# Latent attention over cached pages: score and value products that take four sequences in turn inside each key piece and page

## The reference

```python
def one(args):                                     # one sample
    pt, ql, qp, cn, kn = args
    cp = ckv_pool[pt].reshape(-1, KV_LORA)         # 4096 x 256, also the values
    kp = kpe_pool[pt].reshape(-1, QK_ROPE)         # 4096 x 32
    s_past = (jnp.einsum('qhc,kc->hqk', ql, cp) + jnp.einsum('qhr,kr->hqk', qp, kp)).astype(jnp.float32) * SM_SCALE
...
    p = jax.nn.softmax(jnp.concatenate([s_past, s_new], -1), axis=-1).astype(cp.dtype)
    return (jnp.einsum('hqk,kc->qhc', p[..., :n_past], cp)
            + jnp.einsum('hqk,kc->qhc', p[..., n_past:], cn))
```

## Time and profile before

| | |
|---|---|
| time, median of 3 runs | 4361.26 us (4354.4 to 4364.62) |
| profiled execution: its span | 4359.5 us (1.8 us under the median) |
| mean granted clock of PE in it | 0.927 of full speed |
| PE busy | 88% of the span |
| DVE / POOL / ACT busy | 63% / 35% / 23% |
| latent-attention tiles with page steps | about 660 to 1058 us from the start |

### The profile page before, as it was taken

How to read it: one execution, slowest core, us unless ns; L and a number is a source line. 1 busy time by engine, 2 the same in 40 slices (tenths; PEclk the granted TensorE clock), 3 DMA queues, 4 the chain that set the end, 5 groups by cost and what they waited for, 6 DMA issues and landing times. The chain is left out here.

```text
span 4359.5 us, 50665 instructions
## 1 busy us (share of the span) xinstructions
PE 3848.5 (88%) x17166; PEld 2860.4 (66%) x17166; DVE 2764.4 (63%) x6184; ACT 1006.0 (23%) x2810; POOL 1544.8 (35%) x1332
## 2 busy tenths in 40 slices
PE   9798958888899989989898789977999899898986
PEld 4477844445777767777676545555777777676765
DVE  0255632222599987877776623335999888877777
ACT  0132201121122255431010112211222455310000
POOL 0011213332035365555554200000263655655553
PEclk9888979899999989999999899968999999899998
DMA  3100056775568799999999674404598999999996
GB/s 129 43 15 17 27 161 186 206 205 165 191 247 335 299 400 417 416 410 379 392 395 389 249 255 167 154 19 156 215 343 309 371 416 417 404 387 392 389 398 257
DMA packets 374218, 1168.40 MB, mean 268 GB/s; under 512 B 36914, under 2 KB 163523, under 8 KB 345994
## 3 DMA queue, kind: packets, MB, share of 16 engines
q0 software_dynamic: 159920, 570.80, 34.3%
q1 hardware_dynamic: 187386, 518.08, 32.7%
q10 hardware_dynamic: 26656, 76.29, 4.6%
HBM read 1091.93 MB, written 68.59 MB: 266 GB/s over the span
## 5 line engine op out<-in xcount | busy, mean ns | idle before, releaser
L2046 POOL DMA_INDIRECT peer_ru<-in_u_rows,peer_expert x512 | 797.8, 1558 | 1697.1 <-DVE peer_expert L2426 831.5
L2124 PE MATMUL peer_bank<-peer_xT,peer_u 128*128 128x288 f32 x4096 | 1032.4, 409 | 1.8 <-ACT peer_held L2251 1.8
L2124 PEld LDWEIGHTS peer_bank<-peer_xT,peer_u 128*128 128x128 f32 x4096 | 775.2, 192 | 208.0 <-issue 3.4
L2345 DVE SCALAR_TENSOR_TENSOR y<-peer_rv,peer_weight,y 128x1024 f32<-128x1024 f32 x512 | 656.4, 1282 | 80.2 <-issue 56.5
L2355 DVE CUSTOM_DVE_ANT_0 peer_ru<-peer_ru,x 128x1024 f32<-128x1024 f32 x512 | 623.2, 1217 | 40.7 <-DMA peer_ru<-in_u_rows,peer_expert 40.1
L2054 POOL DMA_INDIRECT peer_rv<-in_v_rows,peer_expert x512 | 536.0, 1047 | 234.2 <-issue 143.6
L2175 PE MATMUL peer_bank<-peer_u,region 128*128 128x288 f32 x1664 | 428.9, 421 | 62.8 <-DMA region<-in_v 62.8
L2175 PEld LDWEIGHTS peer_bank<-peer_u,region 128*128 128x128 f32 x1664 | 328.1, 198 | 161.0 <-DMA region<-in_v 67.4
L2175 PE MATMUL peer_bank<-region,peer_u 128*128 128x288 f32 x1536 | 376.4, 406 | 0.0
L2197 ACT ACTIVATE peer_act_g<-peer_dot 128x1 f32<-128x1 f32 x512 | 103.6, 202 | 1152.9 <-DVE peer_dot L2355 1143.2
L2494 DVE TENSOR_TENSOR peer_hidden<-peer_hidden,peer_bank 128x288 f32<-128x288 f32 x496 | 220.7, 451 | 228.0 <-PE peer_bank L2175 226.5
(11 more groups left out here) (519 smaller groups left out, 4982.2 us busy)
## 6 DMA issues: line engine op xcount, KB each, us to landing
peer_u<-in_uT SPq DMA_DIRECT2D x128, 1024.0 KB, 8.5
peer_u<-in_v SPq DMA_DIRECT2D x32, 2048.0 KB, 12.6
region<-in_v SPq DMA_DIRECT2D x32, 2048.0 KB, 14.2
mlstm_w_in<-in_w_in_o SPq DMA_DIRECT2D x30, 1792.0 KB, 7.3
mla_keys<-in_keysT SPq DMA_DIRECT2D x256, 144.0 KB, 4.8
mla_vals<-in_cache_ckv POOLq DMA_DIRECT2D x256, 128.0 KB, 5.2
peer_held<-in_wq SPq DMA_DIRECT2D x16, 2048.0 KB, 8.4
scratch_early<-peer_hidden ACTq DMA_DIRECT2D x50, 576.0 KB, 9.5
```

Source lines behind the costliest of these rows:

```text
L2046: pool.indirect_dma_start(ru[:, n % U_ROWS, :], None, u_rows, bass.IndirectOffsetOnAxis(ap=expert[:, T, k:k + 1], axis=0)).then_inc(ru_in[ ...
L2124: mm = mmul(bank[:, UNIT_BANKS[i], 0:TD], u[:, h % URING, i % 2, k, :], xT[:, k, :], start=k == 0, stop=k == KD - 1)
L2345: V.scalar_tensor_tensor(out=y[:, T, :], in0=rv[:, n % V_ROWS, :], scalar=weight[:, n:n + 1], in1=y[:, T, :], op0=ALU.mult, op1=ALU.add).t ...
```

## The change

In `scores`, the loop over the three key pieces becomes the outer one and the loop over the four samples the inner one; the waits for the keys of all four samples come ahead of the first matmul. In `values`, the loop over the four pages becomes the outer one and the loop over samples the inner one, with the four waits for values first. The steps over new rows (`j < 0`) get the same order of loops in `scores`. The number and the shapes of the matmuls, the rings, the transfers and the order of the steps stay as they are.

```diff
-                    for b in range(GB):
-                        s = GB * g + b
-                        cols = slice(s * ROWS, (s + 1) * ROWS)
-                        if j < 0:
-                            for k in range(3):
+                    unit = lambda b: (g * JB + j) * GB + b
+                    if j >= 0:
+                        for b in range(GB):
+                            pe.wait_ge(kin[unit(b) % KRING], 16 * JP * (unit(b) // KRING + 1))
+                    for k in range(3):
+                        for b in range(GB):
+                            s = GB * g + b
+                            cols = slice(s * ROWS, (s + 1) * ROWS)
+                            if j < 0:
                                 mm = mmul(bank[b * ROWS:(b + 1) * ROWS, 6, 0:SEG], ...)
-                        else:
-                            n = (g * JB + j) * GB + b
-                            pe.wait_ge(kin[n % KRING], 16 * JP * (n // KRING + 1))
-                            o = bank[b * ROWS:(b + 1) * ROWS, 6, :].rearrange("p (i x) -> p i x", i=JP)
-                            for k in range(3):
-                                mm = mmul(o, qlT[:, k, cols], keys[:, n % KRING, :, k, :], start=k == 0, stop=k == 2)
-                            mm.then_inc(ps, 1)
+                            else:
+                                o = bank[b * ROWS:(b + 1) * ROWS, 6, :].rearrange("p (i x) -> p i x", i=JP)
+                                mm = mmul(o, qlT[:, k, cols], keys[:, unit(b) % KRING, :, k, :], start=k == 0, stop=k == 2)
+                                if k == 2:
+                                    mm.then_inc(ps, 1)
...
+                    unit = lambda b: (g * JB + j) * GB + b
                     for b in range(GB):
-                        ...
-                            n = (g * JB + j) * GB + b
-                            pe.wait_ge(vin[n % RING], 16 * JP * (n // RING + 1))
-                            for i in range(JP):
-                                mm = mmul(o, ppT[:, i, cols], vals[:, n % RING, i, :], start=i == 0, stop=i == JP - 1)
-                            mm.then_inc(gv, 1)
+                        pe.wait_ge(vin[unit(b) % RING], 16 * JP * (unit(b) // RING + 1))
+                    for i in range(JP):
+                        for b in range(GB):
+                            mm = mmul(out(b), ppT[:, i, cols(b)], vals[:, unit(b) % RING, i, :], start=i == 0, stop=i == JP - 1)
+                            if i == JP - 1:
+                                mm.then_inc(gv, 1)
```

More of the change, by code:

```diff
@@ L1301, in values @@
                         pe.wait_ge(new_in, 16 * (g + 1))
-                    for b in range(GB):
[L1303 to L1309, removed]
-                            n = (g * JB + j) * GB + b
-                            pe.wait_ge(vin[n % RING], 16 * JP * (n // RING + 1))
-                            for i in range(JP):
-                                mm = mmul(o, ppT[:, i, cols], vals[:, n % RING, i, :], start=i == 0, stop=i == JP - 1)
-                            mm.then_inc(gv, 1)
+                    out = lambda b: bank[b * ROWS:(b + 1) * ROWS, 0, 0:KV]
+                    cols = lambda b: slice(b * ROWS, (b + 1) * ROWS)
+                    if j < 0:
+                        for b in range(GB):
+                            mm = mmul(out(b), ppT[0:SEG, 0, cols(b)], vnew[:, b, :], start=True, stop=True)
+                        mm.then_inc(s_pv, 1)
+                        return
+                    unit = lambda b: (g * JB + j) * GB + b
+                    for b in range(GB):
+                        pe.wait_ge(vin[unit(b) % RING], 16 * JP * (unit(b) // RING + 1))
+                    for i in range(JP):
+                        for b in range(GB):
+                            mm = mmul(out(b), ppT[:, i, cols(b)], vals[:, unit(b) % RING, i, :], start=i == 0, stop=i == JP - 1)
+                            if i == JP - 1:
+                                mm.then_inc(gv, 1)
                 def group_end(g):
```

## The result

The changed kernel takes 4404.9 us (median of four runs, 4397.5 to 4406.0) against 4357.8 us before (four runs as well, 4345.2 to 4364.6): a ratio of 1.0114, 95% interval 1.0092 to 1.0136. It is slower, as forecast, but by 47 us where 18.6 were worked out; the time lies near the upper end of the range. The profiled execution has a span of 4403.7 us, 44.2 more than before.

The account below looks back on a forecast made before the run. It took the one-step key ring, PE and SP waiting for each other, as the bound: three rounds of 13.8 + 4.3 + 4.46 = 22.6 us per tile, plus tile ends, add 18.6 us, giving 4380 us, range 4347 to 4410.

Parts of the forecast that it names:

- Closed rounds: Three times in each tile SP issues, the last key transfer lands, scores run, SP restarts: 22.6 us a round; chance 0.55.
- issuing: SP issues a step's sixteen key transfers: 13.8 us from the release of the ring place, 1.54 + 12.28.
- The cost of the order on PE: With samples in turn, a step's scores on PE take 2.78 us and its values 2.1, at full clock.
- 13 turns: If samples hold each other back on PE, a step takes 13 turns instead of six: 4465 us; chance 0.05.
- s: Time of a step's scores on PE behind a wait for keys: 4.46 us, bounds 2.78 and 5.33.
- output weights: Two 1024 KB transfers in tiles two to four lengthen one key round of each tile by 1.3 us.
- The tile's end: After a tile's last scores, softmax of 3.5 us and values of 2.1, 5.6 us in all.
- first scores of a tile: A tile's first scores, whose keys are in place: 4.2 us in the first tile, 2.8 in the others.
- L: Landing of a step's last key transfer after SP's issuing ends: 4.3 us, bounds 2.0 and 7.5.
- Case 2: PE's clock holds behind the waits, scores take 2.78 us, 20.2 us go: 4360, no change; chance 0.18.
- Case 3: Keys land as if alone in 2.0 us and output weights hide, 31.5 us go: 4348, faster; chance 0.13.
- Case 4: Keys land as in a full queue, 7.5 us, 38 us more: 4418; chance 0.09.

Follow-up runs that it names:

- e2: The change without the edit of `values`: only the scores take the four samples in turn, with the four waits first; 4407.9 us, 1.0131 to the kernel before.
- e3: The kernel before with its matmul order, only the four waits for keys moved ahead of a step's first score matmul; 4420.5 us, 1.0157 to the kernel before.
- e4: The changed kernel with a key ring of five places instead of four, the fifth lying in `x`; 4356.5 us, 1.0013 to the kernel before.
- e12: The changed kernel itself, run again on another chip; 4402.3 us, 1.0128 to the kernel before.
- e6: The changed kernel with the tile's output weights issued at turn 8 instead of turn 3; 4390.4 us, 1.0092 to the kernel before.
- e11: The changed kernel with twelve extra matmuls ahead of the waits in waiting steps and output weights issued at turn 8; 4371.1 us, 1.0055 to the kernel before.
- e9: The changed kernel with twelve extra matmuls ahead of the waits in waiting steps, seventeen in second rounds of tiles two to four; 4385.5 us, 1.0083.
- e7: The changed kernel, but scores take two samples in turn, then the other two, each pair with its own waits; 4345.7 us, 1.0003 to the kernel before.
- e5: The changed kernel with ten extra matmuls ahead of the four waits in the twelve waiting steps; 4394.0 us, 1.0112 to the kernel before.

## Why the prediction was right about the way and wrong about the size

**The cause held.** Closed rounds, from waits put in one place and places given back together, are what e2, e3 and e4 show. In the changed kernel the round begins in each of the twelve cases with the end of the scores, and issuing takes 13.4 to 15.0 us from there, mean 13.9, where 13.8 was worked out.

**The cost of the order on PE held.** 2.78 and 1.93 us, worked out as 2.78 and 2.1. The rule of the Trainium skill that was weighed there ("TensorE: Matmul & The Clock Gate", Part 3), that matmuls start and end strictly in program order, would, as the prediction read it, have given a step 13 turns. The trace does not agree: six were seen. It does not even hold for the old order: a sample's first score starts 0.89 us after that of the sample before it, with three of whose six still to come, and 3 x 0.89 + 2.76 = 5.43. So samples overlapped there by more than half, and not only at the seams of which the prediction speaks.

**What failed is the size of three terms: the scores behind a wait (s), the output weights, and the tile's end.** For the four tiles together:

| term | predicted us | measured us | short by |
|---|---|---|---|
| first scores of a tile | 4.2 + 3 x 2.8 = 12.6 | 4 x 2.78 = 11.1 | -1.5 |
| issuing | 12 x 13.8 = 165.6 | 166.8 | 1.2 |
| L, without output weights | 12 x 4.3 = 51.6 | 12 x 4.76 = 57.1 | 5.5 |
| output weights, on top of L | 3 x 1.3 = 3.9 | 3 x 3.78 = 11.3 | 7.4 |
| s behind a wait | 12 x 4.46 = 53.5 | 61.0 | 7.5 |
| softmax and last values | 4 x 5.6 = 22.4 | 28.2 | 5.8 |

The last column gives 25.9 us; with the 18.6 forecast that is the 44.5 of the tiles. (L is the start of the scores less the end of SP's sixteenth issue, nine rounds without output weights with a mean of 4.76, three with 10.5, 8.1 and 7.0; s is the sum of the twelve rows above; the end of a tile is from the end of its last scores to that of its last values.) The second profile of the changed kernel, e12, has nearly the same sum, 335.8, and in it 12 x 4.37 = 52.4 for L, 12.8 for the weights, 62.2 for s and 28.6 for the ends. So the miss in L is not steady from one execution to the next; the other three are.

*s*: the prediction took the middle of three rows, on the ground that four samples at once might bring the clock back sooner. They did not: seven of twelve took 5.29 to 5.35 us, the bound from the longest idle. Here the nearest row was at hand, and the reason to leave it was a guess. Case 2, a clock that holds, falls with it. With 5.33 the prediction's own sum gave 4390; most of the rest of the miss is in the other two terms.

*Output weights*: worked out from the mean rate of a full window, as if the key transfers lost only what the sum of bytes asks. They lost three times that: while two transfers of 1 MB are under way the landing of the last key page is late by 3.8 us in the mean. e6 and e11 show that it is these transfers: all three landings fall to 3.1 to 5.3 us when they are issued later. What that is worth in the time, the pair e9 and e11 puts at some 14 us, with runs that scatter over 32 and 38.

*The tile's end*: in the main the clock again. The last values took 3.25, 3.58 and 3.64 us at a granted clock of 0.59, 0.54 and 0.50, and in the fourth tile 1.93 at 1.00; the prediction had charged 2.1 each, the price at full clock. That is 4.0 of the 5.8 us; the other 1.8 lie between the last scores and the values. The window view of the values that end tiles three and four of the kernel after (columns as in the earlier trace rows):

```profile
980.60:984.40 3.80, 3.73 (x33) 1.39 (x32) 0.00 (x0) 0.00 (x0) 0.00 (x0) 0.50 0.53 162
...
1097.60:1099.60 2.00, 1.96 (x33) 0.94 (x32) 0.11 (x1) 0.00 (x0) 0.00 (x0) 1.00 0.00 0
```

Case 3, pages landing as if alone, did not come: the shortest L was 4.3 (3.5 in e12). Case 4, a full queue, came only in the three rounds with output weights.

**Still open.** Of the change's 47 us the rounds' structure is shown by e3 and e4, the clock's part by e9 (17 us of some 28 that it could give) and the weights' part by the landings of e6 and e11 and by e11's time beside e9's. Between e11 and the kernel before 0.55% remain, of which tiles 300.9 - 291.1 = 9.8 us are seen, across two chips, and the rest is not. A wait for each sample, with samples in turn and places given back one by one, was not tried beyond the pairs of e7.

## What to carry to other kernels

When a loop over buffers is moved inside another loop, look first at what the old order did for the transfers: here each buffer was waited for by itself and given back before the next was needed. With a ring of one step, waits put together and releases put together turn that overlap into a round of issue, landing and use, in which saved matmul time counts little; one place more in the ring, or only as many buffers in turn as leave the queue some to fill, opens the round again. And a wait made longer is paid a second time where the engine comes out of it slower: take that price from the row with the nearest idle time, here the 5.33 us after 6.15.

## What the runs showed that was not expected

Four samples side by side behind a wait kept the low clock as long as one sample did: 24 instructions took 5.35 us at a granted clock of 0.50, six of one sample 5.33. The idling ahead of the scores did matter: in e9 1.67 us of it left them at 2.78 us, 4.59 us made them 5.29. But the length of the last pause alone does not decide. The timeline of PE in e9 has a row with a short pause and slow scores:

```profile
732.68 5.35 PE L1284 MATMUL mla_bank<-mla_keys,mla_qlT 96*32 96x512 f32 x24 [2.28 <-DMA mla_keys<-in_keysT]
```

That of e5 has one with a longer pause and fast scores:

```profile
782.24 2.78 PE L1284 MATMUL mla_bank<-mla_keys,mla_qlT 96*32 96x512 f32 x24 [2.83 <-DMA mla_keys<-in_keysT]
```

The timeline of the kernel before already had a row that breaks the rise of the five in the earlier trace rows, full speed after 1.82 us:

```profile
931.19 2.76 PE L1280 MATMUL mla_bank<-mla_keys,mla_qlT 96*32 96x512 f32 x6 [1.82 <-DMA mla_keys<-in_keysT]
```
